# Router product of a two-layer transformer kernel: its weights stationary in two column groups, tokens moving, and a fold behind

## The reference, cut to what matters

```python
def hierarchical_moe(h, wg, bg, we, be, w_gu, w_down):
    hf = h.astype(jnp.float32)
    pg = jax.nn.softmax(hf @ wg.astype(jnp.float32) + bg.astype(jnp.float32), axis=-1)
    gi = jnp.argmax(pg, axis=-1)
    gw = jnp.max(pg, axis=-1, keepdims=True)
    le = (hf @ we.astype(jnp.float32) + be.astype(jnp.float32)).reshape(-1, MOE_GROUPS, MOE_EPG)
    le = jnp.einsum('ng,nge->ne', jax.nn.one_hot(gi, MOE_GROUPS, dtype=jnp.float32), le)
    tw, ti = lax.top_k(jax.nn.softmax(le, axis=-1), MOE_TOPK)
    ...
```

## Time and profile before

| what | us |
|---|---|
| runs, median of 3 | 2758.91 |
| lowest and highest run | 2758.34, 2760.32 |
| span of the profiled execution, first to last instruction | 2754.5 |
| TensorE busy in the span | 2658.7 |
| VectorE busy in the span | 1033.5 |
| ScalarE busy in the span | 544.6 |
| router products L1495, busy, 288 passes | 33.8 |
| output products L1476, busy, 576 passes | 256.1 |

### The profile page before, as it was taken

The page is one execution under the profiler, slowest core; times in us unless marked ns, Lnnn a source line. Parts: engine busy times, 40 slices in busy tenths (PEclk is TensorE's granted clock), DMA queues, the critical chain, the costliest instruction groups (busy, mean ns, idle before and its releaser), DMA issues.

```text
span 2754.5 us, 34258 instructions
## 1 busy us (share of the span) xinstructions
PE 2658.7 (97%) x13616; PEld 1343.9 (49%) x13616; DVE 1033.5 (38%) x2424; ACT 544.6 (20%) x1138; POOL 226.6 (8%) x341
## 2 busy tenths in 40 slices
PE   6999999999989999999999899899999999999996
PEld 3444456556745544433333354477755444444442
DVE  3221337107736642222222362377746511111114
ACT  3211111117811100000000130288821100000001
POOL 0011200003011110000000000000011100000000
PEclk9999999999999999999999999999999999999998
DMA  9641110206060289999998820300030699999996
GB/s 358 253 188 34 35 42 24 73 0 120 2 234 28 92 313 425 428 398 403 415 393 346 339 73 17 63 7 2 2 140 31 254 400 422 421 422 425 423 410 239
DMA packets 97481, 598.77 MB, mean 217 GB/s; under 512 B 17480, under 2 KB 20768, under 8 KB 72360
## 3 DMA queue, kind: packets, MB, share of 16 engines
q1 hardware_dynamic: 83208, 545.15, 50.3%
q0 software_dynamic: 14112, 51.39, 4.6%
HBM read 554.45 MB, written 42.31 MB: 217 GB/s over the span
## 4 chain that ended last, share of the span: by engine, by line
PE 91%; DMA 4%; DVE 2%; issue 1%; SPq 0%; ACT 0%; POOL 0%; PEld 0%; PEldq 0%; DVEq 0%; POOLq 0%; ACTq 0%
PE PS L1818 36%; PE PS L939 24%; PE PS L1476 8%; PE PS L1289 4%; PE PS L1301 4%; PE PS L1312 4%; PE PS L1823 2%; DMA ar<-in_ada_w_dram 1%; PE PS L583 1%; PE PS L1828 1%; PE PS L2223 1%; PE PS L1495 1%; PE PS L1451 1%; DMA ar<-in_x_dram 1%; DMA h2d<-ar 1%
## 5 line engine op out<-in xcount | busy, mean ns | idle before, releaser
L1818 PE MATMUL PS<-ar 128*32 128x512 f32 (+2 forms) x4608 | 1029.7, 594 | 8.7 <-issue 2.9
L1818 PEld LDWEIGHTS PS<-ar 128*32 128x32 f32 (+2 forms) x4608 | 379.0, 138 | 621.4 <-issue 613.0
L939 PE MATMUL PS<-ar 128*128 128x512 f32 (+1 forms) x1600 | 674.4, 578 | 0.2 <-issue 0.2
L939 PEld LDWEIGHTS PS<-ar 128*128 128x128 f32 x1600 | 298.9, 190 | 330.6 <-issue 325.7
L1476 PE MATMUL PS<-ar 128*128 128x512 f32 x576 | 256.1, 598 | 0.6 <-DVEq L420 0.6
L1942 ACT ACTIVATE ar<-PS 128x512 f32<-128x512 f32 x49 | 29.3, 597 | 1065.9 <-PE PS L1818 1065.9
L1343 DVE CUSTOM_DVE_ANT_0 ar<-PS,ar 128x640 f32<-128x640 f32 (+2 forms) x208 | 158.0, 797 | 203.3 <-POOL ar L1259 133.5
L1476 PEld LDWEIGHTS PS<-ar 128*128 128x128 f32 x576 | 107.6, 191 | 123.9 <-issue 123.1
L1398 ACT ACTIVATE ar<-ar 128x641 f32<-128x641 f32 (+4 forms) x208 | 159.5, 772 | 0.8 <-DVE ar L1343 0.8
L2035 DVE TENSOR_TENSOR ar<-PS,ar 128x1024 f32<-128x1024 f32 x49 | 60.0, 1225 | 250.3 <-PE PS L1818 145.2
L2012 DVE TENSOR_TENSOR ar<-PS,ar 128x512 f32<-128x512 f32 x49 | 33.9, 692 | 313.0 <-ACT ar L1942 313.0
(11 more groups left out here) (240 smaller groups left out, 1829.4 us busy)
## 6 DMA issues: line engine op xcount, KB each, us to landing
ar<-in_expert_w_gu_dram SPq DMA_DIRECT2D x128, 2048.0 KB, 14.3
ar<-in_expert_w_down_dram SPq DMA_DIRECT2D x64, 2048.0 KB, 12.0
ar<-in_ada_w_dram SPq DMA_DIRECT2D x24, 2048.0 KB, 13.1
ar<-yd SPq DMA_DIRECT2D x36, 512.0 KB, 7.0
ar<-in_ab_w_in_dram SPq DMA_DIRECT2D x7, 2048.0 KB, 8.7
h2d<-ar SPq DMA_DIRECT2D x18, 512.0 KB, 2.6
ar<-in_swa_w_in_dram SPq DMA_DIRECT2D x3, 2048.0 KB, 8.5
ar<-mod SPq DMA_DIRECT2D x3, 1536.0 KB, 7.8
```

What stands on the lines that cost most here:

```text
L939: mm = nc.tensor.matmul(out_, lhs, rhs, start=(k == 0), stop=(k == KC - 1))
L1818: mm = nc.tensor.matmul(out[at:to], lhsT[:, at:to], w[:, k, cols], start=start, stop=stop)
```

## The change

The router's operands are exchanged. The 36 columns of `rw` become the stationary operand, and the 128 tokens of `h2T` move. Even contraction steps go to array columns 0 to 35 and odd ones to 64 to 99, so that two partial sums of the logits, turned (logits x tokens), stand in `PS[:, 4, P:2P]` on partitions 0 to 35 and 64 to 99. ScalarE copies all 128 partitions of that block to a new tile `lgT`; the block is set to zero once, as the partitions between are never written. One further product, `folded`, has `lgT` as its stationary operand and a constant `fold` of 128 x 36 as the moving one. `fold` is the sum of two shifted identities, so this product both adds the two halves and turns them back to tokens x 36, in the place where the logits stood before. VectorE goes on from there as before.

The order changes too. `router(i - 1)` now stands in the middle of `product(i, 1)`, after four of its eight contraction steps, and `folded(i - 1)` stands where the router was. In the step after the last tile the router stands by itself, with one `running` product between it and the fold. ScalarE's copy is the last part of `evict_h2`, with a wait for the router's semaphore `lt`; its own semaphore is `lc`.

```diff
@@ -1466,13 +1472,15 @@
                     return AO[:, k, at]
                 return mixT[i % 2][:, k, :] if k < 4 else NO[:, k - 4, at]
 
-            def product(i, half):
+            def product(i, half, amid=None):
                 if l == 0:
                     pe.wait_ge(*done(f"{n}_me", i + 1))
                 pe.wait_ge(*done(f"{n}_wo", 16 if l == 0 else 64))
                 if i >= 1:
                     pe.wait_ge(*done(f"{n}_pe", 2 * (i - 1) + half + 1))
                 for k in range(KC):
+                    if amid is not None and k == KC // 2:
+                        amid()
                     mm = nc.tensor.matmul(PS[:, 2 + half, :], mixed(i, k), WO[l][:, k, half * 512:half * 512 + 512],
                                           start=(k == 0), stop=(k == KC - 1))
                 mm.then_inc(S(f"{n}_mm"), 1)
@@ -1489,11 +1497,19 @@
             def router(i):
                 pe.wait_ge(*done(f"{n}_w", 64))
                 pe.wait_ge(*done(f"{n}_he", 2 * i + 2))
+                if i == 0:
+                    pe.wait_ge(*done(f"{n}_fold", 1))
+                for k in range(KC):
+                    at = 64 * (k % 2)
+                    mm = nc.tensor.matmul(PS[at:at + NLOG, 4, P:2 * P], rw[:, k, :], h2T[:, k, :], start=(k < 2), stop=(k >= KC - 2))
+                mm.then_inc(S(f"{n}_lt"), 1)
+
+            def folded(i):
+
+                pe.wait_ge(*done(f"{n}_lc", i + 1))
                 if i >= 1:
                     pe.wait_ge(*done(f"{n}_lg", i))
-                for k in range(KC):
-                    mm = nc.tensor.matmul(PS[:, 4, 0:NLOG], h2T[:, k, :], rw[:, k, :], start=(k == 0), stop=(k == KC - 1))
-                mm.then_inc(S(f"{n}_r"), 1)
+                nc.tensor.matmul(PS[:, 4, 0:NLOG], lgT, fold, start=True, stop=True).then_inc(S(f"{n}_r"), 1)
 
             def ranks(i):
 
@@ -1524,9 +1540,12 @@
                 if i >= 2:
                     ranks(i - 2)
                 if i < len(ts):
-                    product(i, 1)
+                    product(i, 1, (lambda: router(i - 1)) if i >= 1 else None)
+                elif i == len(ts):
+                    router(i - 1)
+                    running(1)
                 if 1 <= i <= len(ts):
-                    router(i - 1)
+                    folded(i - 1)
                 if i == len(ts) + 1:
                     running(1)
                 if i >= 2:
@@ -1555,11 +1574,13 @@
 
             def evict_h2(i):
                 if i >= 1:
-                    act.wait_ge(*done(f"{n}_r", i))
+                    act.wait_ge(*done(f"{n}_lt", i))
                 for half in range(2):
                     act.wait_ge(*done(f"{n}_ht", 2 * i + half + 1))
                     nc.scalar.activation(h2T[:, 4 * half:4 * half + 4, :].rearrange("p k n -> p (k n)"), PS[:, 6 + half, :], ACT.Copy)\
                         .then_inc(S(f"{n}_he"), 1)
+                act.wait_ge(*done(f"{n}_lt", i + 1))
+                nc.scalar.activation(lgT, PS[:, 4, P:2 * P], ACT.Copy).then_inc(S(f"{n}_lc"), 1)
             if l == 0:
                 evict_mix(0)
                 evict_mix(1)
@@ -1657,6 +1678,8 @@
                 last.then_inc(S(f"{n}_pos"), 1)
                 dve.wait_ge(*done(f"{n}_pos", i + 1))
 
+            V.memset(PS[:, 4, P:2 * P], 0.0)
+            V.tensor_tensor(fold, ident[:, 0:NLOG], ident[:, 64:64 + NLOG], ALU.add).then_inc(S(f"{n}_fold"), 1)
             for i, t in enumerate(ts):
                 if l == 0:
                     dve.wait_ge(*done("o0_x_in" if t < XT else "o0_ctx_in", 16))
```

More of the change, by code:

```diff
@@ L226, in program @@
         onp = [[R(TR + 2432 + 256 * i + 128 * j, P) for j in range(2)] for i in range(2)]
+        lgT = R(TR + 2944, P)
         mixT = [R(TR + 3072 + 512 * i, 512).rearrange("p (k n) -> p k n", k=4) for i in range(2)]
@@ L252, in program @@
         hbias, rstd = R(RT + 320, NT), R(RT + 330, NT)
+        fold = R(RT + 344, NLOG)
         rhs = [R(RT + 384 + 128 * i, 128).rearrange("p (j n) -> p j n", j=2) for i in range(2)]
@@ L308, in program @@
         share(("{}_mt", "{}_me"), "o0", "o1", NT)
+        share(("{}_lt", "{}_lc"), "o0", "o1", NT)
+        share(("{}_fold",), "o0", "o1", 1)
+        for before, after, total in (("core_s", "o0_lt", NT), ("core_x", "o0_lc", NT), ("states", "o0_fold", 2)):
+            share(("{}",), before, after, total)
         share(("{}_r", "{}_lg", "{}_rt", "{}_M", "{}_rank", "{}_rk", "{}_pos", "{}_acc", "{}_sb"), "o0", "o1", NT)
```

## The result

The changed kernel takes 2764.11 us (median of 22 runs, lowest 2762.33), the kernel before 2759.65 beside it (22 runs). Two of the 22 were slow runs (2857.72 and 7170.48 us, at a mean granted clock of 0.934 and 0.485); the ratio leaves them out, and the median of the others is 2763.96. The ratio is 1.0015, with a 95% interval of 1.0009 to 1.0022: 4.5 us slower by the medians, between 2.5 and 6.1. The changed kernel is slower beyond its interval, by a little less than the 0.2% that the prediction took for the edge. The forecast was +5.5 us. The profiled executions span 2754.5 us before and 2760.5 after.

The account below looks back on a forecast made before the run. TensorE bound the kernel by a narrow margin, with 1.1 us of slack to VectorE's choices. Layer 1 +3.33, layer 0 +0.98, tails +0.80 and clock +0.40 made +5.51: 2764.4 us, 8 in 10 from 2758.5 to 2769.

Parts of the forecast that it names:

- The choices end the wait: At `ranks`, in both layers: TensorE now waits for VectorE's choices, T0 + 8.94; rival that they do not bind: 0.12.
- R: What the new router adds to TensorE where it stands: 1.21 us, 0.85 for eight pairs and 0.36 for the column groups.
- Periods: Time from one tile to the next: 17.57 us in both layers, against 17.29 in layer 1 and 17.68 in layer 0.
- Fold: The added product where the router stood, two passes with 128 stationary columns: 0.21 us on TensorE.
- The layers: The two stretches of `out_pe` up to the last tile: +0.98 us in layer 0, +3.33 in layer 1.
- T0: The moment when TensorE is through with issuing a tile's second half product; arrivals at `ranks` are counted from it.
- The wait of 0.15 us for the eviction: Layer 0, product from 811.95: the router waits 0.15 us for the eviction, part of +1.36 there.
- The tails: After each layer's last tile: +0.80 us for the last routers and +0.40 for the clock.
- the longer last router: In each tail, the last router to its logits takes 2.51 us instead of 2.11: +0.40 a layer, +0.80 together.
- the clock: In the tails, longer TensorE idle time before the last turns extends the 1.2 GHz level: +0.4 us.
- My own case: The whole kernel at 2764.4 us with the choices binding and R at 1.21: chance 0.68, own range 2762.5 to 2767.

Follow-up runs that it names:

- e: The changed kernel with two more small VectorE instructions in each chain of choices, their results unused: 2771.42 us, ratio 1.0045 to the kernel before.
- f: The kernel before with two more small VectorE instructions in each chain of choices, their results unused: 2760.85 us, ratio 1.0004 to the kernel before.
- c: The changed kernel with `ranks` moved into the middle of the second half product, just ahead of the router: 2759.00 us, ratio 0.9995 to the kernel before.
- a: The kernel before with its old router moved into the middle of the second half product, no fold: 2771.64 us, ratio 1.0040 to the kernel before.
- b: The changed kernel with all eight contraction steps of the router in one column group: 2778.22 us, ratio 1.0070 to the kernel before.
- d: The changed kernel with the router back behind the second half product and the fold inside the next half product: 2754.37 us, ratio 0.9980 to before.

## Why the prediction was right, point by point

**The choices end the wait.** Right, and shown four ways: `ranks` idles for L1659 in each of the six tiles of layer 1 before the tail (0.99 us once, then 0.37 or 0.38 by the profile, 0.53 from the end of issue at 2065.77, where about 0.5 was forecast); a longer chain of choices costs its length after the change and nothing in a tile before (e, f); with `ranks` moved out of the way the period falls to 16.84 us (c); the move alone, without the new router, costs 11.6 us (a).

**R.** Forecast 1.21, measured 1.20. b shows the bound for passes in a row: 3.61 + 1.87 + 3.54 - 6.95 = 2.07, the forecast 2.07. But the 0.35 us over the eight pairs is not all what the prediction took it for. The router of before, moved into the middle of the product (a), adds 3.52 + 1.70 + 3.51 - 6.95 = 1.78, which is 0.08 more than its own 1.70. And the new router behind the product (d) adds about 1.11: 8.04 us for product and router (2076.69 to 2084.73) less 6.95, and 0.02 in the passes behind. So some 0.26 us belongs to the column groups, less than the 0.36 taken from attention, and 0.09 to standing between 512-column passes, which had no term. That the two came to the forecast sum is luck.

**Periods.** Forecast 17.57 in both layers, measured 17.56 and 17.57.

**Fold.** Forecast 0.21, measured 0.14 (2057.36 to 2057.50). It was mis-sized, as the first of its two loads runs under the pass ahead, which L1510 behind another short product cannot show. It changed nothing, since it lies in front of a wait. The slack which the wait took back is larger by it.

**The layers.** From the first product that ranks released (811.95 before, 811.00 after) to T0 of the last tile (944.05, 943.89), layer 0 takes 132.10 us before and 132.89 after: +0.79, forecast +0.98. The wait of 0.15 us for the eviction did not show: the router starts at 816.40, straight behind 5.40 us of product, and the eviction had ended at 815.97. In layer 1, from the first product (2008.57, 2009.99) to T0 of the last tile (2140.30, 2145.18), it is 131.73 and 135.19: +3.46, forecast +3.33. The first period is 17.73 us (2039.63 to 2057.36), 0.16 over the forecast 17.57: the sum had left out the memset in the first chain of choices, behind which `ranks` idles 0.99 us.

**The tails.** This is the term that was mis-sized. Forecast were +0.80 for the longer last router and +0.40 for the clock, 1.20 together. From T0 of the last tile to the first expert product it took 30.25 and 29.65 us before (944.05 to 974.30, 2140.30 to 2169.95) and takes 29.99 and 30.09 after (943.89 to 973.88, 2145.18 to 2175.27): -0.26 and +0.44, together +0.18. The first expert product in layer 0 and in layer 1 before, and in layer 1 after:

```profile
974.30 7.13 PE L1818 MATMUL PS<-ar 128*128 128x512 f32 x16 [0.46 <-DVE ar L2005]
```

```profile
2169.95 7.13 PE L1818 MATMUL PS<-ar 128*128 128x512 f32 x16 [0.46 <-DVE ar L2005]
```

```profile
2175.27 7.13 PE L1841 MATMUL PS<-ar 128*128 128x512 f32 x16 [0.46 <-DVE ar L2028]
```

The tail in four stretches, each with its length in us and the mean granted clock:

| stretch | layer 0 before | layer 0 after | layer 1 before | layer 1 after |
|---|---|---|---|---|
| T0 of the last tile to the last turns | 3.74, 1.00 | 3.74, 1.00 | 3.74, 0.91 | 3.73, 1.00 |
| last turns to last router | 5.79, 0.71 | 5.77, 0.70 | 6.87, 0.55 | 5.78, 0.70 |
| last router to last `ranks` | 6.80, 1.00 | 7.07, 1.00 | 6.96, 0.75 | 7.07, 1.00 |
| last `ranks` to first expert product | 13.92, 0.75 | 13.41, 0.75 | 12.08, 1.00 | 13.51, 0.75 |

The longer last router costs 0.27 and 0.11 us up to `ranks`, 0.38 together and not 0.80. The last logits come 2.38 us behind its start (953.40 to 955.78) instead of 2.11, where 2.51 was forecast: the `running` product and the fold behind it start 0.97 us apart, which had been put at 1.07 with the way out of the groups.

```profile
955.78 0.20 DVE L1634 TENSOR_TENSOR ar<-PS,ar 128x36 f32<-128x36 f32 x1 [0.39 <-PE PS L1512]
```

In layer 1 only 0.11 of this was left, as before the change the warming passes at the lower clock had held `ranks` up for 0.15 us.

The clock was to cost 0.40; the other stretches give back 0.20. TensorE idles 2.96 us before the last turns, as forecast, and yet the next stretch is no colder, in layer 1 even warmer: it is 1.09 us shorter. In layer 0 the twelve warming passes of the last stretch take 7.30 us instead of 7.80. But in layer 1 the last stretch fell from 1.00 to 0.75 and takes 1.43 us more, as its twelve warming passes, before and after, show:

```profile
2161.06 5.40 PE L1451 MATMUL PS<-cst 128*128 128x512 f32 x12
```

```profile
2165.66 7.40 PE L1457 MATMUL PS<-cst 128*128 128x512 f32 x12
```

Over the whole tail the mean granted clock is 0.83 in both layers, before and after: the lower level moved, and did not grow. The working of that term was also wrong in itself, for 2.3 us of work at full clock takes 4.6 us at half of it, 2.3 more and not 1.1. With 0.18 in place of 1.20, +5.5 became 0.79 + 3.46 + 0.18 = 4.4, close to what the medians differ by (4.5). This sum is of one profiled execution of each kernel. Their spans differ by 6.0: the parts outside these stretches differ as well, by -0.9, +1.8 and +0.7 us, 1.6 together. So the closeness of 4.4 is in part luck.

**The chances.** My own case has come true; it stands within 0.2% because of the tails. The changed kernel's two halves, taken apart, have opposite signs: the new router with its fold in a good place gains 5.7 us (d), the move loses 11.6 (a). These add up to +5.9 where 4.5 was measured, which the intervals of the three allow. The two layers, 4.25 of the 4.4 us, came out within 0.06 us of the forecast and for the reason given; the tails were put 1.0 us too high.

## What to carry to other kernels

A product shortened on the engine that is busy all the time gains only the slack that the next engine has in the same loop: write down, from one common moment, when each engine arrives at each wait, and see which wait ends last after the edit. An edit in two parts, here a cheaper instruction and a new place for it, is priced part by part; the place can cost more than the instruction saves. Work put ahead of the product that others wait for delays all of them by its full length, while the same work behind it is free up to their slack.

## What the runs showed of the hardware

Passes of 36 stationary columns in the column groups at 0 and 64 run two by two as those of 64 do: 16 in 1.00 us against 1.87 in one group. Going into the groups and back costs some 0.26 us (d); in the middle of a chain of 512-column passes it is 0.35, of which a router without column groups pays 0.08 there too (a). An idle time of 0.4 us in each 17.6 us did not touch the granted clock (1.00). Behind 5.16 us of idle time in one piece, the next 7.01 us had a granted clock of 0.63 (c). In the tails the length of the idle time did not tell how cold the stretch behind it would be: 1.40 us went before one at 0.55 and before one at 0.71, 2.96 us before two at 0.70, and over the whole tail it was 0.83 each time.
